# Norm sums folded over groups of 32 output columns, with roots on fewer columns and spreading products, in a two-block fp32 kernel

## What is computed

```python
def rms_norm(x, g):
    y = xf * lax.rsqrt(jnp.mean(jnp.square(xf), axis=-1, keepdims=True) + EPS)
    return (y * g.astype(jnp.float32)).astype(x.dtype)
...
kk = kk * lax.rsqrt(jnp.sum(kk * kk, axis=-1, keepdims=True) + 1e-12)       # RWKV-7, 8 heads of 64
y = ((y - mean) * lax.rsqrt(var + RWKV_GN_EPS)).reshape(B, L, MIX_W) * ln_w + ln_b
o = o * lax.rsqrt(jnp.mean(o * o, axis=-1, keepdims=True) + 1e-5) * norm_g   # GLA, 4 heads of 128
```

## Time and profile before

| | us |
|---|---|
| median of 3 runs | 1868.67 |
| lowest and highest | 1866.36, 1868.9 |
| the profiled execution | 1868.79 |
| its span in the trace | 1866.7 |

### The profile page before, as it was taken

How to read it: one execution, slowest core, us unless ns; L and a number is a source line. 1 busy time by engine, 2 the same in 40 slices (tenths; PEclk the granted TensorE clock), 3 DMA queues, 4 the chain that set the end, 5 groups by cost and what they waited for, 6 DMA issues and landing times.

```text
span 1866.7 us, 25902 instructions
## 1 busy us (share of the span) xinstructions
PE 1766.2 (95%) x10456; PEld 1393.1 (75%) x10456; DVE 907.7 (49%) x1725; ACT 406.8 (22%) x771; POOL 295.9 (16%) x305
## 2 busy tenths in 40 slices
PE   7999999899999999899899999988999899999997
PEld 5434454488888888656899996856798688888886
DVE  1247542464675444575587643187711432255511
ACT  1312453221012210346222002221421101200000
POOL 0100252122002211005233110066000000000000
PEclk9999999999999999999999999889999999999999
DMA  7775492122233222321345454232312343244443
GB/s 290 290 294 200 159 346 107 68 86 76 110 135 113 90 78 82 111 68 48 133 167 173 164 179 140 92 110 106 114 55 84 118 153 135 91 158 157 142 152 113
DMA packets 38703, 256.22 MB, mean 137 GB/s; under 512 B 4128, under 2 KB 7328, under 8 KB 9024
## 3 DMA queue, kind: packets, MB, share of 16 engines
q1 hardware_dynamic: 36240, 240.86, 36.6%
q0 software_dynamic: 1776, 9.57, 1.4%
q10 hardware_dynamic: 576, 4.19, 0.5%
HBM read 247.27 MB, written 7.34 MB: 136 GB/s over the span
## 4 chain that ended last, share of the span: by engine, by line
PE 80%; DVE 12%; ACT 2%; issue 2%; POOL 2%; DMA 2%; SPq 0%; ACTq 0%; DVEq 0%; POOLq 0%
PE ps L595 79%; DVE arena L1873 1%; PE ps L790 1%; DMA ring<-weights 1%; DVE arena L2031 1%; DMA xT<-x_t 1%; POOL aux L1676 0%; DVE aux L1903 0%; DVE arena L1904 0%; DVE arena L1905 0%; ACT hT L1322 0%; DVE arena L2070 0%; POOL aux L1659 0%; DVE spare L2143 0%; POOL hT L1719 0%
## 5 line engine op out<-in xcount | busy, mean ns | idle before, releaser
L595 PE MATMUL ps<-hT,ring 128*128 128x256 f32 (+3 forms) x3184 | 744.1, 392 | 22.6 <-issue 17.0
L595 PEld LDWEIGHTS ps<-hT,ring 128*128 128x128 f32 (+1 forms) x3184 | 574.6, 194 | 182.3 <-issue 112.6
L595 PE MATMUL ps<-arena,ring 128*128 128x256 f32 (+3 forms) x1884 | 380.4, 358 | 5.0 <-DVE arena L1905 3.2
L595 PEld LDWEIGHTS ps<-arena,ring 128*128 128x128 f32 (+1 forms) x1884 | 317.6, 190 | 59.0 <-issue 13.7
L1659 POOL TENSOR_TENSOR aux<-aux 128x256 f32<-128x256 f32 (+1 forms) x46 | 50.1, 1088 | 611.0 <-ACT aux L1257 542.9
L595 PE MATMUL ps<-arena,sums 128*128 128x256 f32 (+1 forms) x768 | 136.5, 327 | 1.3 <-DVE aux L1969 1.3
L595 PEld LDWEIGHTS ps<-arena,sums 128*128 128x128 f32 x768 | 118.2, 191 | 12.3 <-DVE aux L1969 2.5
L1257 ACT ACTIVATE aux<-xT 128x256 f32<-128x256 f32 (+1 forms) x64 | 30.9, 494 | 285.7 <-DVE xT L2061 93.3
L1676 POOL TENSOR_SCALAR aux<-aux,small 128x512 f32<-128x512 f32 (+1 forms) x48 | 70.9, 1485 | 113.6 <-DVE small L1921 113.4
L1695 POOL TENSOR_TENSOR arena<-arena 128x256 f32<-128x256 f32 (+1 forms) x32 | 27.0, 843 | 332.6 <-ACT arena L1442 332.6
L595 PE MATMUL ps<-hT,sums 128*128 128x128 f32 (+1 forms) x512 | 78.6, 302 | 0.7 <-DVE aux L1969 0.4
(11 more groups left out here) (335 smaller groups left out, 1817.1 us busy)
## 6 DMA issues: line engine op xcount, KB each, us to landing
ring<-weights SPq DMA_DIRECT2D x224, 1024.0 KB, 4.9
kept_turns<-aux ACTq DMA_DIRECT2D x4, 1024.0 KB, 5.6
arena<-kept_turns POOLq DMA_DIRECT2D x6, 512.0 KB, 4.9
kept_keys_values<-spare POOLq DMA_DIRECT2D x1, 2048.0 KB, 10.2
arena<-kept_keys_values POOLq DMA_DIRECT2D x1, 2048.0 KB, 8.2
tab<-tables SPq DMA_DIRECT2D x1, 1344.0 KB, 13.7
arena<-mem_t SPq DMA_DIRECT2D x2, 512.0 KB, 5.6
xT<-ctx_t SPq DMA_DIRECT2D x1, 1024.0 KB, 9.2
```

The costliest lines, as they stand in the source:

```text
L595: ins = nc.tensor.matmul(o_, lhsT, rhs, start=start, stop=stop, skip_group_check=True)
```

## The change

`fold` multiplies by 32 columns of ones: the sums of tokens 128i to 128i+127 land in partitions 32i to 32i+31 of one 128-column block. Root and reciprocal then run on 128 columns (`folded_root`, `inverse`) in a tile `roots`. `spread` multiplies a column of the identity, broadcast over 128 columns, with `roots`, so that the inverse of each group comes back on 128 partitions in a second bank (pool hold), from which VectorE multiplies (J and K copy it to `rinv` first). For G, H and I `four_sums` folds four tiles of 256 tokens (in H and I two heads in each), and `four_spread` takes two banks of the run pool. `gla_end` moves to behind tiles 1 and 2, with G's reciprocal behind tile 0. In A, J and K the spreading products stand behind some products of the next matrix.

```diff
...
@@ -643,6 +645,24 @@
+            def token_tiles_of(s):
+                return range(s.start // P, s.stop // P)
+            def fold(key, src, tiles, first, last, c0=0):
+                for i, t in enumerate(tiles):
+                    mm(bank(key)[32 * i:32 * i + 32, c0:c0 + P], ones[:, 0:32], src[:, t * P:(t + 1) * P], first, last,
+                       key if last and t == tiles[-1] else None)
+            def spread(key, name, tiles, c0=0):
+                o_ = open_bank(key, "hold")
+                pe.wait_ge(S["inverse"], INVERSES.index(name) + 1)
+                rows = 32 * len(tiles)
+                for i, t in enumerate(tiles):
+                    mm(o_[:, t * P:(t + 1) * P], table("ident")[0:rows, 32 * i:32 * i + 1].to_broadcast([rows, P]),
+                       roots[0:rows, c0:c0 + P], True, True, key if t == tiles[-1] else None)
@@ -651,10 +671,16 @@
                     pe.wait_ge(S["square_sums"], SUM_ORDER.index(norm) + 1)
-                    mm(bank(key)[:, s], ones, sq[:, 0, s], True, False)
-                    return
-                pe.wait_ge(S["squares"], KD * norm + (2 * k + 2 if norm == 4 else k + 1))
-                mm(bank(key)[:, s], ones, sq[:, k, s], False, k == K - 1, key if k == K - 1 else None)
+                else:
+                    pe.wait_ge(S["squares"], KD * norm + (2 * k + 2 if norm == 4 else k + 1))
+                first, last, i = k == n_sum - 1, k == K - 1, 0 if k == n_sum - 1 else k
+                if norm == 4:
+                    fold(key, sq[:, i, :], (0, 1), first, False)
+                    fold(key, sq[:, i, :], (2, 3), False, last, P)
+                elif norm:
+                    fold(key, sq[:, i, :], token_tiles_of(s), first, last)
+                else:
+                    mm(bank(key)[:, s], ones, sq[:, i, s], first, last, key if last else None)
@@ -826,10 +852,14 @@
                 wo_early(0)
-                stat(("cvar", l), 2, lambda k: ctmp[:, k, s], lambda k: pe.wait_ge(S["conv_centred"], 2 * l + k + 1),
-                     n=s.stop - s.start, c0=s.start)
+                open_bank(("cvar", l), "hold")
+                for k in range(2):
+                    pe.wait_ge(S["conv_centred"], 2 * l + k + 1)
+                    fold(("cvar", l), ctmp[:, k, :], token_tiles_of(s), k == 0, k == 1)
+                    if n == 1:
+                        spread(("cvb", l), f"conv{l}", token_tiles_of(s), P)
...
@@ -901,6 +932,11 @@
                     stat_of_x(n)
+                if l == 0:
+                    spread(("nb", 2), 2, range(4))
+                else:
+                    spread(("nb", 4), 4, (0, 1))
+                    spread(("nbx", 4), "x1", (0, 1), P)
@@ -1029,11 +1065,29 @@
                 rw_tile(i)
+            def four_sums(key, src, lhsT):
+                o_ = open_bank(key, "hold")
+                for i in range(4):
+                    mm(o_[32 * i:32 * i + 32, 0:T], lhsT, src[:, i, :], True, True, key if i == 3 else None)
+            def four_spread(name, inverse, columns):
+                m = P // len(columns)
+                for half in range(2):
+                    key = (name, half)
+                    o_ = open_bank(key)
+                    if half == 0:
+                        pe.wait_ge(S["inverse"], INVERSES.index(inverse) + 1)
+                    for a in range(2):
+                        for n, c in enumerate(columns):
+                            row = 32 * (2 * half + a) + c
+                            mm(o_[n * m:(n + 1) * m, a * T:(a + 1) * T], table("ident")[:, row:row + 1].to_broadcast([P, m]),
+                               roots[:, :], True, True, key if a == 1 and c == columns[-1] else None)
-                key = ("gos", hh)
-                o_ = open_bank(key, "hold")
-                mm(o_[:, :], ones, g_osq[:, 2 * hh:2 * hh + 2, :].rearrange("p a t -> p (a t)"), True, True, key)
+            four_sums(("gos",), g_osq, ones[:, 0:32])
@@ -1045,6 +1099,8 @@
                 s5_filler(2 * m)
+                if m == 0:
+                    four_spread("glab", "gla", (0,))
@@ -1070,8 +1126,11 @@
             pe.wait_ge(S["rw_act"], 1)
-            head_sums("kks", r_b)
-            gate_tiles(3)
+            pair_of_heads = table("headones")[:, 48:80]
+            four_sums(("kks",), r_b, pair_of_heads)
+            gate_tiles(1)
+            four_spread("kkb", "rw_k", (0, 16))
+            gate_tiles(2)
@@ -1184,10 +1243,12 @@
             pe.wait_ge(S["rw_act"], 5)
-            head_sums("rv", r_e)
+            four_sums(("rv",), r_e, pair_of_heads)
+                if (n, b) == BRANCH_ORDER[1]:
+                    four_spread("rvb", "rw_y", (0, 16))
@@ -1207,6 +1268,8 @@
                 plain("xq", 0, n, ("xq", n), ready=(lambda k: pe.wait_ge(S["h2_ready"], KD + k + 1)) if n == 0 else None)
+                if n == 0:
+                    spread(("nb", 6), 6, (2, 3))
...
@@ -1260,6 +1326,12 @@
                 did(f(dst[:, s], bank(key)[:, s], ACT.Sqrt, bias=table(eps), scale=scale), key=key)
+            def folded_root(key, rows, scale, eps="eps6", c0=0, n=P, a=0):
+                finished(act, key)
+                did(f(roots[0:rows, c0:c0 + n], bank(key)[0:rows, a:a + n], ACT.Sqrt, bias=table(eps)[0:rows, :], scale=scale),
+                    key=key)
...
@@ -1607,12 +1677,11 @@
                 did(f(flat2(r_e, half), flat2(r_y, half), ACT.Square), "rw_act")
-            for half in range(2):
-                rooted(("rv", half), flat2(r_b, half), 1.0 / RD, "epsgn")
+            folded_root(("rv",), P, 1.0 / RD, "epsgn", n=T)
-            root(("st", 6), rinv, xs, 1.0 / D)
+            folded_root(("st", 6), 64, 1.0 / D)
...
@@ -1750,12 +1819,20 @@
-            def scaled(norm, s, key, name="scaled"):
-                taken(dve, key)
-                did(v.reciprocal(rinv[:, s], rinv[:, s]))
+            def inverse(rows, c0=0, n=P):
+                r = roots[0:rows, c0:c0 + n]
+                did(v.reciprocal(r, r), "inverse")
+            def done_with(key):
+                did(v.memset(small2[:, 18, 0:1], 0.0), key=key)
+            def scaled(s, key, name="scaled", free=True):
+                finished(dve, key)
-                    did(v.tensor_tensor(hT[:, k, s], xT[:, k, s], rinv[:, s], ALU.mult), name, wait=False)
+                    did(v.tensor_tensor(hT[:, k, s], xT[:, k, s], bank(key)[:, s], ALU.mult), name, wait=k == KD - 1)
+                if free:
+                    done_with(key)
...
@@ -1930,9 +2012,11 @@
                 taken(dve, ("cvar", l))
-                did(v.reciprocal(rinv2[:, s], rinv2[:, s]))
+                inverse(64 if l else P, P)
+                finished(dve, ("cvb", l))
-                    did(v.tensor_tensor(conv[:, k, s], conv[:, k, s], rinv2[:, s], ALU.mult), "conv_scaled")
+                    did(v.tensor_tensor(conv[:, k, s], conv[:, k, s], bank(("cvb", l))[:, s], ALU.mult), "conv_scaled")
+                done_with(("cvb", l))
...
@@ -2027,27 +2113,29 @@
-            def recip(a):
-                did(v.reciprocal(a, a))
-            did(ts(rinv2[:, 0:T], bank(("st", 4))[:, xs], EPS, D * EPS * EPS, ALU.mult, ALU.add))
-            did(tt(rinv2[:, 0:T], bank(("st", 4))[:, 0:T], rinv2[:, 0:T], ALU.add), "x1_square")
+            did(ts(roots[0:64, 0:P], bank(("st", 4))[0:64, P:2 * P], EPS, D * EPS * EPS, ALU.mult, ALU.add))
+            did(tt(roots[0:64, 0:P], bank(("st", 4))[0:64, 0:P], roots[0:64, 0:P], ALU.add), "x1_square")
-            recip(rinv2[:, 0:T])
+            inverse(64)
+            taken(dve, ("st", 4))
+            inverse(64, P)
+            finished(dve, ("nb", 4))
-                did(stt(hT[:, k, xs], xT[:, k, xs], both[:, k:k + 1], rinv2[:, 0:T], ALU.mult, ALU.mult), "h2_ready", wait=False)
-            taken(dve, ("st", 4))
-            recip(rinv[:, xs])
+                did(stt(hT[:, k, xs], xT[:, k, xs], both[:, k:k + 1], bank(("nb", 4))[:, 0:T], ALU.mult, ALU.mult), "h2_ready",
+                    wait=k == KD - 1)
+            done_with(("nb", 4))
+            finished(dve, ("nbx", 4))
-                did(stt(xT[:, k, xs], xT[:, k, xs], col("final_norm_g", 0, k), rinv[:, xs], ALU.mult, ALU.mult))
+                did(stt(xT[:, k, xs], xT[:, k, xs], col("final_norm_g", 0, k), bank(("nbx", 4))[:, 0:T], ALU.mult, ALU.mult))
+            done_with(("nbx", 4))
@@ -2111,11 +2199,11 @@
             def gla_end(hh):
-                taken(dve, ("gos", hh))
-                r = flat2(page(8), hh)
-                recip(r)
+                key = ("glab", hh)
+                finished(dve, key)
+                r = bank(key).rearrange("p (a t) -> p a t", a=2)
-                did(stt(y, g_o[:, 2 * hh:2 * hh + 2, :], col("gla_norm_2"), page(8)[:, 2 * hh:2 * hh + 2, :], ALU.mult, ALU.mult))
+                did(stt(y, g_o[:, 2 * hh:2 * hh + 2, :], col("gla_norm_2"), r, ALU.mult, ALU.mult), key=key)
@@ -2145,8 +2233,11 @@
                     rw_tile(n)
-                if n in (4, 8):
```

(40 more changed lines are left out.)

39 lines of the change are left out of this document (25 added, 14 removed).

## The result

The changed kernel takes 1872.41 us (median of 12 runs, 1868.92 to 1874.45), the kernel before in the same runs 1866.62 (1863.45 to 1869.0): a ratio of 1.0024, 95% interval 1.0016 to 1.0033. It is slower, by 4.5 us (3.0 to 6.2) by the ratio. The measured median lies inside the forecast range of 1859 to 1873, but the time moved the other way.

The account below looks back on a forecast made before the run. TensorE works 95% of the span, so shorter VectorE or ScalarE operations pay only where it stands still, and added products cost full time. The places sum to −2.75 us from 1868.79: 1866.0, range 1859 to 1873.

Parts of the forecast that it names:

- C: Place with sums for x and the context: shorter TensorE pause avoids 1.2 us of half-clock cost, chain −0.3; −1.5 in all.
- G: Tiles of S5: new TensorE pauses for banks, the pauses for states vanish; +2 us, bounds −2 and +6.5.
- J and K: Two places where TensorE works on through the root: spread of 4 records paid, less the fold's saving; +0.3 us each.
- F: Place where four records take 3.45 us at half clock: shorter chain, clock gives back 0.7; −1.6 us, bounds −2.5 and −0.5.
- D: Place where TensorE is busy with other products: fold saves, spread adds, half of each of A's; +0.2 us.
- B: Place where TensorE stands for root and reciprocal: fold, root, reciprocal save, spread and hand-overs add; −1.8 us, half-clock stretch stays.
- H: Place with one gate tile as cover: fold −0.8, spread +1.9, wait 0.5, removed reciprocals hidden; +1.6 us, bounds +1.0 and +2.8.
- I: Place where TensorE stands 3.86 us before the first gated sum: pause is split, half clock avoided; −1.6 us, bounds −1.9 and 0.
- the second: At G, VectorE's wait for the root makes TensorE stand 6.5 us, later pauses remain: +6.5 there, 1874.0 total; chance 0.15.
- The fourth: At the folds: they don't overlap, 32-column records cost as 128-column ones; about +7 us, 1873; chance 0.03.
- the third: At VectorE's multiplications: reading the inverse from PSUM costs some 65 ns each, 40 reads, +2.6 us, 1868.6; chance 0.05.
- Rival 1: S5 stage gets faster as the early stall is taken up: G −4.9 in place of +2, 1859.1 us; chance 0.18.

Follow-up runs that it names:

- run 7: Kernel before with six one-column memsets on VectorE ahead of its reading of F's sums, nothing folded: 1866.84 us, ratio 0.9997; G's stretch 97.56.
- runs 4 and 8: Both against the changed kernel: 4 adds useless products in TensorE's pauses at B and C, 1870.54 us; 8 splits C's spread in two parts, C's stretch 88.38.
- run 2: Changed kernel with G's reciprocal, spread and gla_end moved later in the S5 loop: 1860.62 us, ratio 0.9966 to the kernel before; G's stretch 91.20.

## Why the prediction was wrong

The steps that failed are C's avoided half clock (2.3 us off), G's sum (2.1), the spread of J and K (0.9 for both), F (0.7) and D (0.5). The other places came within 0.4.

Per place: the forecast, and the mean over traces with the place folded less the mean over those without. There are five or more of either, but only three without F and four without I and L. G stands for the four traces with its parts early against the two of before:

| | A | B | C | D | E | F | G | H | I | J, K | L |
|---|---|---|---|---|---|---|---|---|---|---|---|
| forecast | −0.1 | −1.8 | −1.5 | +0.2 | −0.3 | −1.6 | +2.0 | +1.6 | −1.6 | +0.6 | −0.25 |
| measured | −0.05 | −1.6 | +0.8 | +0.7 | −0.4 | −0.9 | +4.1 | +1.3 | −2.0 | +1.5 | −0.2 |

The sum is about +3.2, against 3.0 to 6.2 by the timed runs and −2.75 forecast. G's +4.1 isn't the worth of its edit alone: with F folded the unchanged G takes 96.8 us, and against that the edit costs 7.5.

- **G, the step "+2, with bounds −2 and +6.5", was mis-sized by 2.1.** The order of events was right: a pause for tile 1's bank, forecast 6.5 to 7.6, measured 8.05; one for tiles 4 and 5, 5.5 and 5.72; and no wait over 2 us for the states. The sizes were not. The two pauses came to 13.8 in place of 13.1. The smaller waits grew from about 2.4 us to 4.7, where the term "a later end of VectorE's last tile" had 1.5. TensorE's work grew by 1.5, where spread, fold and half clock had 0.9. "TensorE needs about 9.4 us a pair" is right by itself: from 1262.67 to 1282.87 it works 18.84 us on two pairs. But these take 20.2, with a wait of 0.6 to 0.8 before each `s5_out`, and VectorE and GpSimd are busy for 17.05 and 17.67 of them. No engine is full; they wait for one another, so the stalls put ahead aren't recovered. And of what I meant to win back, some 3.4 us of G's 100.3 go away with another order of VectorE and GpSimd and more full clock (run 7). One of the held-up additions I had seen in the timeline, at 3.13 us, and left out.
- **C, "I take 1.2 of the half-clock cost as avoided", did not come.** I took a shorter pause for a safer clock. The clock fell for 6.8 or 10.2 us in the folded traces and for 0 to 6.8 in the others. C's stretch is 87.4 to 88.4 us folded and 85.9 to 88.1 not, so that a loss of 0.8 on the mean is likely, and the forecast gain of 1.5 isn't seen. The fold makes TensorE's own work shorter ahead of the pause and puts the spread, at twice its price, into it; which of the two lowers the clock is open. The 0.3 I summed for the chain was therefore also wrong: the spread was priced at 1.0 and takes 2.04 at B and C, and 2.17 in place of 0.9 at F.
- **B** came out near its −1.8 on the mean, at −1.6, and at 0 in the profiled trace, where a second stretch at half clock ate it. The step "the half-clock stretch stays" holds in most of the others, with 6.8 us; one has 10.2 and the one with useless products 3.4.
- **J, K and D: the spread inside running work costs about 0.8, not 0.5**, and the fold saves 0.1 at J: +0.75 for each of J and K, forecast 0.3. From 1552.42 to 1556.71 the 16 records of the matrix and the four of the spread take 4.29 us, where such 16 records alone take 3.45. So the spread costs 0.84, where the sum had four times 0.1255:

```profile
1552.42 3.72 PE L597 MATMUL ps<-hT,ring 128*128 128x256 f32 x16
1556.07 0.71 PE L597 MATMUL ps<-roots,tab 64*128 64x128 f32 x4
1556.71 9.55 PE L597 MATMUL ps<-hT,ring 128*128 128x256 f32 x43
```

- **F** rested on one trace with 3.45 us for four records; in the second trace of before they take 1.98. The 0.7 that the clock should have given back did not come: it fell for 10.2 us in every folded trace.
- **H** right: +1.3 with VectorE's next wait, for ScalarE's L1641, 6.18 us behind the last multiplication, so that the reciprocals had indeed been hidden:

```profile
1343.44 1.23 DVE L2269 TENSOR_TENSOR arena<-arena 128x1024 f32<-128x1024 f32 x1 [6.18 <-ACT arena L1641]
```

- **I** was better than its bound of −1.9, at −2.3, in seven of nine traces: no half clock, and the gated sum is ready when TensorE comes. In the other two (runs 4 and 8) a half-clock stretch of 3.4 us falls on the spread, and −1.2 is left.
- A spread of 64 rows out at 0.12 a record was right (1.95 for 16). The folds on 256 columns cost less than their rows said, 0.64 for 8 records against 1.05.

Of the rivals, the second ("the wait for G's root") is the one that happened, with the first half of its mechanism; its price was +6.5 at G, which is too high; C indeed gave nothing and F little, while I kept its gain. The fourth is refuted by the folds' 0.43; the third by 479 to 480, and in the changed trace a multiplication with a PSUM source takes as long as before (4.87 for eight, 4.90 before). Rival 1, the gain of 4.9 at G, did not come in the change; with the parts placed later, run 2 has 9.

## What to carry to other kernels

Taking 5 us of reciprocals off a row of work is worth it only where their input is ready: put the consumer of another engine's result behind the point at which that result has arrived, and count who stands behind the bank that the waiting engine holds. A round trip through TensorE in one of its pauses cost twice its price here (2.04 us for 1.0), and a shorter pause did not bring the full clock back. Take two traces of the kernel before as the ground for a term under 2 us: a stretch that differs between them is no price.
